# Products of constants in TensorE's waits of a one-core transformer step: 62 added, none read

## The reference, cut to what matters

```python
for l in range(DEPTH):                       # two layers
    m = _adaln(cond, ada_w[l], ada_b[l])     # silu(cond) @ w + b, split in 6
    h = _modulate(_rms(x, norm_mix[l]), m[0], m[1])
    if l == 0:   o = latent attention (8 heads) and short convolution, then w_o
    else:        o = pointwise 1024->2048, GLU, 31-tap convolution, LayerNorm, silu, pointwise
    x = x + m[2] * o
    h = _modulate(_rms(x, norm_ffn[l]), m[3], m[4])
    if l == 0:   f = _swiglu(h, ffn_gu, ffn_down)          # dense, width 2816
    else:        f = _moe(h, router, moe_gu, moe_down)     # top 2 of 8 experts, width 3584
    x = x + m[5] * f
```

## Time and profile before

| | us |
|---|---|
| three runs | 1577.27, 1578.24, 1578.58 (median 1578.24) |
| the profiled execution, its own time | 1578.13 |
| its span, from the first to the last instruction | 1576.3 |
| mean granted TensorE clock over the span | 0.975 of 2.4 GHz |
| PE busy | 1504.0 (95%) |
| DVE busy | 1194.9 (76%) |
| ACT busy | 969.1 (61%) |

### The profile page before, as it was taken

How to read it: one execution, slowest core, us unless ns; L and a number is a source line. 1 busy time by engine, 2 the same in 40 slices (tenths; PEclk the granted TensorE clock), 3 DMA queues, 4 the chain that set the end, 5 groups by cost and what they waited for, 6 DMA issues and landing times.

```text
span 1576.3 us, 22550 instructions
## 1 busy us (share of the span) xinstructions
PE 1504.0 (95%) x8346; PEld 1263.9 (80%) x8346; DVE 1194.9 (76%) x1195; ACT 969.1 (61%) x989; POOL 22.7 (1%) x28
## 2 busy tenths in 40 slices
PE   5979989999999879999999999999999999999997
PEld 2858789998887768888888888888888888888885
DVE  2547564444798568889879889888988997988996
ACT  2436253432547357777776777777777777776773
POOL 0110000000000000000000000000000000000000
PEclk9989999999999879999999999999999999999999
DMA  9654586665744429989989998998998998998993
GB/s 364 253 218 176 176 299 222 226 202 192 263 161 161 161 84 373 374 338 355 372 340 357 374 363 330 371 378 323 370 374 323 372 373 323 370 375 322 372 374 132
DMA packets 100877, 468.56 MB, mean 297 GB/s; under 512 B 8108, under 2 KB 38972, under 8 KB 51664
## 3 DMA queue, kind: packets, MB, share of 16 engines
q1 hardware_dynamic: 99408, 464.81, 78.4%
q10 hardware_dynamic: 864, 1.76, 0.3%
q0 software_dynamic: 544, 1.15, 0.2%
HBM read 466.55 MB, written 1.14 MB: 297 GB/s over the span
## 4 chain that ended last, share of the span: by engine, by line
PE 90%; DVE 4%; DMA 2%; ACT 2%; issue 1%; POOL 0%; SPq 0%; ACTq 0%; DVEq 0%
PE bank L1507 20%; PE bank L1505 20%; PE bank L1506 20%; PE bank L1511 6%; PE bank L1512 5%; PE bank L1513 5%; PE bank L1522 2%; PE bank L1935 2%; DMA raw<-ada_w 2%; PE bank L1835 2%; PE bank L1963 2%; PE bank L1790 1%; PE bank L1791 1%; PE bank L1792 1%; DVE hid L1248 1%; PE bank L1537 1%
## 5 line engine op out<-in xcount | busy, mean ns | idle before, releaser
L1401 DVE TENSOR_TENSOR low<-raw,high 128x2048 fp32r<-128x2048 f32 x333 | 748.5, 2289 | 118.3 <-ACT high L784 113.6
L784 ACT ACTIVATE high<-raw 128x2048 fp32r<-128x2048 f32 x333 | 626.6, 1920 | 75.3 <-DMA raw<-moe 70.6
L1505 PE MATMUL bank<-high,hidH 128*128 128x512 f32 x896 | 350.9, 392 | 3.1 <-ACT hidL L774 3.1
L1507 PE MATMUL bank<-high,hidL 128*128 128x512 f32 x896 | 349.9, 391 | 0.0
L1506 PE MATMUL bank<-low,hidH 128*128 128x512 f32 x896 | 349.5, 390 | 0.0
L1511 PE MATMUL bank<-hidH,high 128*128 128x256 f32 x736 | 213.4, 290 | 16.3 <-DVE hidL L912 5.1
L1512 PE MATMUL bank<-hidL,high 128*128 128x256 f32 x736 | 210.9, 287 | 0.0
L1513 PE MATMUL bank<-hidH,low 128*128 128x256 f32 x736 | 210.7, 286 | 0.0
L1505 PEld LDWEIGHTS bank<-high,hidH 128*128 128x128 f32 x896 | 168.7, 188 | 38.0 <-ACT hidL L774 3.5
L1507 PEld LDWEIGHTS bank<-high,hidL 128*128 128x128 f32 x896 | 168.6, 188 | 35.2
L1506 PEld LDWEIGHTS bank<-low,hidH 128*128 128x128 f32 x896 | 168.7, 188 | 34.7
(11 more groups left out here) (225 smaller groups left out, 1381.2 us busy)
## 6 DMA issues: line engine op xcount, KB each, us to landing
raw<-moe SPq DMA_DIRECT2D x336, 1024.0 KB, 4.8
raw<-ada_w SPq DMA_DIRECT2D x48, 1024.0 KB, 6.1
raw<-ffn_gu SPq DMA_DIRECT2D x44, 512.0 KB, 5.0
raw<-ffn_down SPq DMA_DIRECT2D x11, 1024.0 KB, 7.1
raw<-w_in SPq DMA_DIRECT2D x8, 1024.0 KB, 10.2
raw<-conv_pw SPq DMA_DIRECT2D x16, 512.0 KB, 5.2
raw<-w_o SPq DMA_DIRECT2D x4, 1024.0 KB, 6.2
raw<-conv_pw SPq DMA_DIRECT2D x4, 1024.0 KB, 5.3
```

The lines of the kernel that those rows point to most:

```text
L784: a.activation(high[:, m % SPLITS, :], raw[:, n % RAWS, :], ACT.Copy).then_inc(S("high_ready"), 1)
L1401: v.tensor_tensor(low[:, n % RAWS, :], raw[:, n % RAWS, :], high[:, m % SPLITS, :].bitcast(F32), ALU.subtract).then_inc(S("low_ready"), 1)
L1505: pe.matmul(out, xh, wh, start=start, stop=False)
L1507: return pe.matmul(out, xl, wh, start=False, stop=stop)
```

## The change

A helper `spare(b, c0, n)` is added, which issues `n` plain float32 products of the identity with the first 256 columns of the constants (128x128 times 128x256) into columns `c0` to `c0 + 255` of bank `b`, each with start and stop. Nobody reads what they write, and they signal nothing. It is called at 16 places in the text: 62 products run in all. No wait and no other instruction is changed.

```diff
+            def spare(b, c0, n):
+                for _ in range(n):
+                    pe.matmul(bank[:, b, c0:c0 + 2 * P], ident, const[:, 0:2 * P], start=True, stop=True)
...
             ada_sum(0)
+            spare(3, 0, 4)
...
             for k in range(3):
                 ada_piece(1, k)
+            spare(3, 0, 4)
...
                 for half in range(2):
+                    if i == 1 and half:
+                        spare(1, 0, 3)
...
             ada_sum(1)
+            spare(3, 0, 7)
             chunk(("win", 3, 1), 4, pairs_of(4), None, False, {}, 0)
             heads_transposed(4)
+            spare(6, 2 * P, 2)
...
             norm_sum(1, 3)
             ada_sum(2)
+            spare(3, 0, 2)
             ada_piece(3, 0)
...
                 unit_product(("ffn", "b", u), 4, 2, None if u else split_ready(1))
+                if u == 0:
+                    spare(7, 0, 7)
...
             ada_piece(4, 0)
+            spare(3, 0, 6)
             norm_sum(2, 2)
...
             for k in range(KT):
                 pe.wait_ge(S("ln_sq"), k + 1)
                 last = tile_sums(sq[:, k, :], 4, 0, k == 0, k == KT - 1)
+                if k < KT - 1:
+                    spare(3, 0, 1)
             st.mark(last, "ln_ssum")
+            spare(3, 0, 2)
             broadcast(bank[:, 5, 0:TOK], TILES, 12)
             ada_sum(5)
+            spare(4, 0, 2)
...
             chunk(("pw2", 1, 1), 4, pw2_out(1), None, True, {(1, KH - 1): "out_pair"}, 0)
+            spare(4, 0, 3)
             norm_sum(3, 2)
             norm_sum(3, 3)
+            spare(4, 0, 3)
             broadcast(bank[:, 7, TOK:2 * TOK], TILES, 14)
+            spare(4, 0, 2)
...
             x_transposed(0)
+            spare(7, 2 * P, 4)
             pe.wait_ge(S("slots_read"), 1)
...
                 gather(0)
                 if not passes:
                     x_transposed(1)
+                    spare(3, 0, 4)
                 gate_up_first(0)
```

## The result

| | median us | range | executions |
|---|---|---|---|
| kernel before | 1578.41 | 1577.27 to 1578.99 | 4 |
| changed kernel | 1565.26 | 1563.01 to 1566.86 | 4 |

The change takes 13.2 us off by medians. The ratio is 0.9918, 95% interval [0.9903, 0.9934]. The profiled execution took 1564.23 us, with a span of 1562.4 (13.9 under the span of before).

A forecast was written before the change was run, and what follows sets the result against it. PE holds 90% of the chain of waits and loses time at half clock after waits. Place-by-place gains sum to 15.5 us, less 4.5 for three remaining falls: gain 11.0, from 1578.13 to 1567 us, range 1561.5 to 1576.

The forecast's parts named there:

- rival A: Whole kernel: each set of spares holds the clock to the next work; gain over 13.5, about 1563 us; chance 0.20.
- A spare product costs 0.45 us at full clock, 0.9 at half: All sets: price of one 256-column product, taken from `ln_sums`; 62 make 28 us of PE work, hidden where waits are longer.
- the calls without a row: Three calls of 2 or 3 products in waits of about their own size: put at nothing, up to a microsecond each at low clock.
- 0.44 of a stretch of dense work: Dense PE work at clock 0.50: loss per stretch, from equal 48-product chunks taking 5.83 and 7.62 us, 1.79 us lost over 4.05.
- routing: Gather 3.3, the 8 transposes behind it 0.8, first expert's start 1.8: together 5.9 us gained at full clock.
- The LayerNorm's seven products cost 3.1: Between the LayerNorm's eight `tile_sums`, where PE has no wait: 7 x 0.45 = 3.1 us added to the path.
- First chunk: nothing gained, and a stand 1.5 longer before 45.5: First input chunk at 36.97: full clock would give 1.5 us, but PE then waits for DVE's last `hidL`.
- Three falls remain, 4.5 us: Five thin places named; three falls of the clock expected to stay, each 3.4 us x 0.44 = 1.5, so 4.5 off.
- The span from the first expert to the end stays 997 us: Expert phase: sign of being right, first expert's start to the end unchanged at 997 us; a longer phase a sign of wrong.
- term of 1.8 for the first expert's products: First expert, 578.98 to 583.02: 4.04 us at 0.50 x 0.44 = 1.8 us gained.
- The rule I set aside: Whole kernel: falls placed anew in each run, times scattering by a few; not used, since three runs lay within 1.3 us.
- Rival D: Whole kernel: spares don't hold the clock and their cost stands alone; 4.2 us slower, about 1582 us; chance 0.09.

The follow-up runs named there:

- e1: The kernel before with only the two routing sets added, four products after each x_transposed: 1576.06 us, kernel before 1580.00, ratio 0.9976.
- e6: The changed kernel with sets refitted to its waits, most longer, and none among the LayerNorm sums: 1563.51 us, kernel before 1579.63, ratio 0.9902.
- e3: The changed kernel without the seven products among the LayerNorm sums: 1560.38 us, kernel before 1580.00, ratio 0.9886.
- e5: The changed kernel again, unedited, beside the kernel before on another chip: 1564.86 us, kernel before 1579.63, ratio 0.9901.
- e10: The changed kernel once more, unedited, in the last group of runs: 1564.30 us, kernel before 1580.65, ratio 0.9902.
- e4: The changed kernel with the same 62 products cut from 256 columns to 2: 1581.61 us, kernel before 1580.00, ratio 1.0014.

## Why the prediction was right, and where it was not

Forecast 1567.0 (gain 11.0, range 1561.5 to 1576.0), measured 1565.3 (13.2), and 1564.3 to 1565.3 in the three groups. The three traces of the changed kernel have spans 13.9, 12.9 and 13.1 us below before's. By medians beside the kernel before of the same chip the gain was 13.2, 14.8 and 16.4: the last two lie in the band of rival A (over 13.5), since the kernel before was slower there (1579.6, 1580.7). The intervals don't separate the forecast's band from A's. By its steps:

- *A spare product costs 0.45 us at full clock, 0.9 at half.* Right: 1.89 us for four, and 3.37 where the clock was at 0.50. The sets lie in the waits; of the calls without a row the one behind the third `ada_sum` (172.81) costs 0.3.
- *0.44 of a stretch of dense work, and the sizes of the terms.* The 0.44 rests on a stretch of low clock that the earlier trace rows leaves out, in the windows view of before:

```profile
105.15:111.98 6.83, 4.05 (x19) 4.06 (x20) 2.78 (x4) 0.00 (x0) 0.00 (x0) 0.50 0.82 342
```

  Right to a few tenths: queries 1.5 (lead -0.9 to 0.6), keys and values 1.6, the chunk 1.8, scores 1.6 (I had 1.4), unit 1 1.3, RMSNorm 2.0 (1.8), broadcast and `pw2` 1.9 (1.9), sums ahead of the router 1.7 (1.5), routing 5.7 to 6.0 in three traces (5.9; e1 alone 5.1). With the LayerNorm's place as measured the terms add up to some 16.7, where the forecast had 15.5.
- *The LayerNorm's seven products cost 3.1.* The sign right, the size 2.5: they kept the clock for the last groups of sums themselves, which had run at 0.50 (the 32 records take 3.73 us in e6 at full clock, 4.27 in the earlier trace rows). The balance that I gave with it (-1.2) was -0.6, and e3 shows it from the other side: without them the place is 0.5 faster.
- *First chunk: nothing gained, and a stand 1.5 longer before 45.5.* Right, and this thin place did fall: in five of six traces with this set alone, for 1.4 us at the broadcast of 64 us. By the traces the set is a loss there; the times don't settle it.
- *Three falls remain, 4.5 us.* About right as a mean: two, four and five falls in three traces. The first trace lost 1.4 us to the one at 45 and little to the one that its spares met; e5 reached the second piece of the first expert 3.2 us later than that, and e10 3.7. So the number is a mean over executions and no constant of the kernel. Where falls came was partly named (45, the sums around 543 to 549, the routing) and partly not: the heads at 93, `ada_w` at 175.
- *The span from the first expert to the end stays 997 us.* This sign contradicts the forecast's own term of 1.8 for the first expert's products, which lie inside the span. The span did stay (997.5), by luck, for two reasons that cancel: 1.9 us less in the first piece, and 2.9 us more in the experts' loop less 0.9 at the end. In e5, with the loop as before, it is 995.3, which is what the term of 1.8 asks for. An expert phase with a longer loop was named as a sign of being wrong; it came in this one execution.
- *The rule I set aside.* This was the misjudgement. "TensorE: Matmul & The Clock Gate" of the Trainium skill, Part 1, says that what decides over the clock "doesn't reset when your kernel starts". I held three executions within 1.3 us against it. The runs agree with the page: the same kernel shows two, four and five stretches of 0.50, and the kernel before spreads over 9.6 us in 53 executions. Three executions on one chip were too few to see it. The agreement has a limit: e5's and e10's falls coincide, and the traces of before and e1 have theirs at the same places up to 400 us, two of them with other lengths. It changes no term of the sum, but it makes "how many falls" a chance at every thin wait rather than a property of the kernel, and A and the forecast lie in one scatter.
- *Two slips in the sums.* D's price of 4.2 leaves out the half microsecond that it names (3.1 + 0.6 + 0.5 + 0.5 = 4.7), and what was put low is 1.2 in one place and 1.1 in another. Neither moves a bound by more.

Rival D had a true core, e4: where the added products hold no clock, nothing is gained. Rival A's full sum was there in the first trace up to the first expert (15.9), though no median of the changed kernel came to 1563 or below. What stays open: why the experts took 0.31 us more each in one execution of thirteen, with PE at 1.00 and without waits. It is not the program's instructions (e5 and e10 are the same ones), and it did not come again.

## What to carry to other kernels

Filling PE's waits with products that nobody reads is worth what the low clock costs behind each wait, and the places can be counted one by one: here 0.44 us for each microsecond of dense work that follows at 0.50. Put them where PE waits for something that the products don't delay. Leave room for a set that has to run at half clock (e6: five took 4.06 us and lost what they should have won); a set that exactly fills its wait at full clock has none. Among instructions that the path goes through they cost their length (2.5 us here, for 1.9 back). And judge such a change by many executions: a wait that keeps its clock in one trace loses it in the next.

## What the runs showed of the hardware

- The stretches at 0.50 are not a property of the kernel alone: the changed kernel had them at 44.94 and 553.52 us in one trace, at 45.74, 93.53, 175.45 and 540.68 in another, and at these four (to 0.03 us) and 557.72 in a third.
- With 62 products of 2 columns the clock was at 0.50 in ten stretches ahead of the experts, 20.5 us of it in the routing (e4); with the same 62 of 256 columns in two, four and five stretches, at most 3.4 us of it in the routing.
- One execution ran the whole loop over the experts 0.25% slower (123.73 us instead of 123.42 an expert) at a granted clock of 1.00, by steps of 0.02 us at the same products of each expert.
